# The gate-spreading stage of a PEER decoder layer: first factors made by three engines instead of two

## The chip, the cores and the metric

The kernel runs on one core of a Trainium2 chip. The metric is the device time of one execution, in microseconds (us). Before the change the median of three runs is 3275.36 us (3272.27 to 3279.01). One further execution was profiled; it took 3269.89 us, and its trace is what the rows below come from.

## The reference, cut to what matters

One decoder layer on 1024 tokens: attention (two kinds of heads), then a PEER channel mixer, then a norm. In the mixer each token picks, in each of 8 heads, 16 experts out of 128 x 128. An expert is a pair of keys (i1, i2), and each pick has a gate.

```python
best, flat = lax.top_k(cand.reshape(cand.shape[0], PEER_HEADS, PEER_TOPK * PEER_TOPK), PEER_TOPK)
...
expert = i1 * PEER_NKEYS + i2
gate = jax.nn.softmax(best, axis=-1)
...
act = jax.nn.gelu(jnp.einsum('td,thkd->thk', tc, u_sel).astype(jnp.float32), approximate=False)
return jnp.einsum('thk,thkd->td', (act * gc).astype(tc.dtype), v_emb[ec])
```

The kernel computes the mixer for the last 576 tokens (`TD`) densely, over all 16384 experts. For that it needs, for each of these tokens, a 128 x 128 table of gates that is zero except at the token's 128 picks.

## The kernel before, in words

The program is a row of stages, each with its own instruction streams for TensorE, VectorE, ScalarE, GpSimd and SyncE: projection in, attention, projection out, routing (`route`), the spreading of the gates (`spread_gates`), and the experts (`run_experts`). The change lies in `spread_gates` alone.

`slotT` holds for each dense token three columns over 128 partitions, one partition for each pick: the first key, the second key and the gate. The gate table of a token is the product of two 128 x 128 factors over the picks: `first[pick, i] = gate * (i == first key)` and `second[pick, j] = (j == second key)`. TensorE multiplies them (L1579), one f32 matmul for each token, into PSUM.

The 576 tokens are handled in 72 groups of eight (`OCT`), in a fixed order on every engine. A group of eight goes like this:

- VectorE makes `one` (L1552), the bf16 comparison of a row of numbers `iota_gb` with the first keys, laid out with the token innermost, for all eight tokens. Then `second` (L1557), the f32 comparison with the second keys, 1024 elements. Then `first` for the last four tokens (L1562), `one` times the gate.
- ScalarE makes `first` for the first four tokens (L1589), one instruction for each token, reading `one` with a step and scaling by the gate. It runs one group ahead, and then copies the finished group from PSUM to `gates` (L1599).
- GpSimd does nothing in this stage.

The buffers `one`, `first` and `second` are threefold (`BUFS`), the PSUM banks fourfold. VectorE waits for `first_act` and `first_dve` of three groups ago before `one`, and for the matmuls of three groups ago (`spread_done`) before `second`. TensorE waits for the group's `second_ready`, `first_dve` and `first_act`.

The gate tables leave SBUF in five tiles of 64, 128, 128, 128 and 128 tokens, in two alternating buffers. SyncE sends the first four as each is complete (L1527, after 8, 24, 40 and 56 groups). It then waits for the fourth to land and issues six loads for the next stage: `u_raw` twice, `hn_hi_e`, `hn_lo_e`, `v_raw` twice (L1530 to L1536). The fifth tile is sent after group 72, in two parts: 8 of its 128 columns by SyncE (L1539) and the other 120 by ScalarE (L1612). In `run_experts` SyncE waits for the second part before it loads `rows`, `early`, `tail`, `gain` and the next `v_raw`, and GpSimd waits for it before it starts.

Of the kernel before, what the change touches and what calls it, by code (L numbers as in the profile page):

```python
# [6 lines left out]
P = 128  # L7
# [22 lines left out]
PH, NKEY, PQ, TOPK = 8, 128, 256, 16  # L30
# [32 lines left out]
bf16 = mybir.dt.bfloat16  # L63
i32 = mybir.dt.int32
u32 = mybir.dt.uint32
ALU = mybir.AluOpType
# [1411 lines left out]
def spread_gates(core, slotT, outer):  # L1478

    nc, ps = core.nc, core.ps  # L1480
    OCT = 8
    TU = BANK // NKEY
    NB = OCT // TU
    BUFS = 3
    PS_BUFS = 4
    EDGES = [0, *range(P - HALF_AT, TD + 1, P)]
    NOCT = TD // OCT
    ON_ACT = 4
    LEAD = 8
    with ExitStack() as ctx:  # L1490
        sb, new_sem = core.scope(ctx)
        made = []

        def sem(name):
            made.append(new_sem(name))
            return made[-1]

        with nc.sbuf_tensor("gates1", [P, NKEY, P], f32, side="right") as gates1:
            pass
        lead = Lead(core, outer)  # L1500
        gates = [ctx.enter_context(nc.sbuf_tensor("gates0", [P, NKEY, P], f32, side="right")), gates1]
        one = sb("one", [P, BUFS, NKEY, OCT], bf16)
        first = sb("first", [P, BUFS, OCT, NKEY])
        second = sb("second", [P, BUFS, OCT, NKEY])
        iota_f = core.iota
        iota = sb("iota_gb", [P, NKEY, OCT], bf16)
        keysT = sb("slot_keys", [P, TD], bf16)
        iota_ready, keys_ready = sem("iota_ready_g"), sem("keys_ready_g")
        one_ready, second_ready, first_act, first_dve = (sem(x) for x in (
            "one_ready", "second_ready", "first_act", "first_dve"))  # L1510
        spread_done, gates_out = sem("spread_done"), sem("gates_out")
        sent = [sem(f"gates_sent{k}") for k in range(2)]
        clear_counts(nc, (*made, *lead.semaphores()))
        block = ctx.enter_context(nc.Block())
        flat = slotT

        def need(eng, sem_, value):
            if value > 0:
                eng.wait_ge(sem_, value)

        @block.sync
        def _(sp):
            dst = core.scr_g.rearrange("j i t -> i j t")
            for tile in range(NDT - 1):
                a, b = EDGES[tile], EDGES[tile + 1]
                sp.wait_ge(gates_out, b // OCT)
                sp.dma_start(dst[:, :, a:b], gates[tile % 2][:, :, 0:b - a]).then_inc(sent[tile % 2], 16)  # L1527
            assert NDT % 2 == 1
            sp.wait_ge(sent[1], 16 * (NDT // 2))
            sp.dma_start(lead.u_raw[:, 0, :], core.i["uT"][0]).then_inc(lead.u_in[0], 16)  # L1530
            sp.dma_start(lead.u_raw[:, 1, :], core.i["uT"][1]).then_inc(lead.u_in[1], 16)
            sp.dma_start(lead.hn_hi[:, :, :].bitcast(f32), core.scr_hi).then_inc(lead.hn_in, 16)
            sp.dma_start(lead.hn_lo[:, :, :].bitcast(f32), core.scr_lo).then_inc(lead.hn_in, 16)
            v_v = core.i["v_rows"].rearrange("(i j) d -> j i d", j=NKEY)
            for c in range(CH):
                sp.dma_start(lead.v_raw[:, c, :], v_v[c]).then_inc(lead.v_in[c], 16)  # L1536
            sp.wait_ge(sent[0], 16 * (NDT // 2))
            sp.wait_ge(gates_out, NOCT)
            sp.dma_start(dst[:, 0:LEAD, EDGES[-2]:], gates[0][:, 0:LEAD, :]).then_inc(lead.last_sent[0], 16)  # L1539

        @block.vector
        def _(dve):
            nc.vector.tensor_copy(iota[:, :, :], iota_f[:, :].rearrange("p (i o) -> p i o", o=1)
                                  .to_broadcast([P, NKEY, OCT])).then_inc(iota_ready, 1)
            nc.vector.tensor_copy(keysT[:, :], flat[:, 0, :]).then_inc(keys_ready, 1)
            dve.wait_ge(iota_ready, 1)
            dve.wait_ge(keys_ready, 1)
            for n in range(NOCT):
                b, at = n % BUFS, n * OCT
                need(dve, first_act, n - BUFS + 1)  # L1550
                need(dve, first_dve, n - BUFS + 1)
                nc.vector.tensor_tensor(  # L1552
                    one[:, b, :, :], iota[:, :, :],
                    keysT[:, at:at + OCT].rearrange("p (o t) -> p o t", o=1).to_broadcast([P, NKEY, OCT]),
                    ALU.is_equal).then_inc(one_ready, 1)
                need(dve, spread_done, n - BUFS + 1)
                nc.vector.tensor_tensor(  # L1557
                    second[:, b, :, :], iota_f[:, :].rearrange("p (o i) -> p o i", o=1).to_broadcast([P, OCT, NKEY]),
                    flat[:, 1, at:at + OCT].rearrange("p (t o) -> p t o", o=1).to_broadcast([P, OCT, NKEY]),
                    ALU.is_equal).then_inc(second_ready, 1)  # L1560
                dve.wait_ge(one_ready, n + 1)
                nc.vector.tensor_tensor(  # L1562
                    first[:, b, ON_ACT:, :], one[:, b, :, ON_ACT:].rearrange("p i t -> p t i"),
                    flat[:, 2, at + ON_ACT:at + OCT].rearrange("p (t o) -> p t o", o=1)
                    .to_broadcast([P, OCT - ON_ACT, NKEY]), ALU.mult).then_inc(first_dve, 1)
            for c in range(CH):
                lead.split_u(nc, dve, c)

        @block.tensor
        def _(pe):  # L1570
            for n in range(NOCT):
                b, bank = n % BUFS, NB * (n % PS_BUFS)
                pe.wait_ge(second_ready, n + 1)
                pe.wait_ge(first_dve, n + 1)
                pe.wait_ge(first_act, n + 1)
                need(pe, gates_out, n - PS_BUFS + 1)
                for t in range(OCT):
                    slot = ps[:, bank + t // TU, :].rearrange("p (i t) -> p t i", t=TU)[:, t % TU, :]
                    last = nc.tensor.matmul(slot, first[:, b, t, :], second[:, b, t, :], start=True, stop=True)  # L1579
                last.then_inc(spread_done, 1)  # L1580

        @block.scalar
        def _(act):
            def weight(n):
                b, at = n % BUFS, n * OCT
                act.wait_ge(one_ready, n + 1)
                need(act, spread_done, n - BUFS + 1)
                for t in range(ON_ACT):
                    last = nc.scalar.activation(first[:, b, t, :], one[:, b, :, t], ACT.Copy,  # L1589
# [645 lines left out]
def layer(nc, ins, out):  # L2235
    with ExitStack() as ctx, ExitStack() as outer:
# [24 lines left out]
        with ExitStack() as peer:  # L2261
            eid = peer.enter_context(nc.sbuf_tensor("eid", [P, GT, 2, UNIT], i32))
            eidT = peer.enter_context(nc.sbuf_tensor("eidT", [P, GT, P], i32))
            sgate = peer.enter_context(nc.sbuf_tensor("sgate", [P, GT, 2, UNIT], f32))
            slots = peer.enter_context(ExitStack())
            slotT = slots.enter_context(nc.sbuf_tensor("slotT", [P, 3, TD], f32))
            route(core, hn_hi, hn_lo, w_raw, keys, slotT, eid, eidT, sgate)
            hidden.close()
            lead = spread_gates(core, slotT, peer)
            slots.close()  # L2270
            run_experts(core, eid, eidT, sgate, lead)
# [52 lines left out]
```

## Time and profile before

| what | value |
|---|---|
| median of 3 runs | 3275.36 us |
| profiled execution | 3269.89 us |
| its span | 3268.1 us |
| TensorE busy | 2969.7 us (91%) |
| VectorE busy | 2194.5 us (67%) |
| ScalarE busy | 991.5 us (30%) |
| GpSimd busy | 1262.3 us (39%) |
| matmuls of `spread_gates`, first and last start | 1173.9 and 1368.5 us |

The engines' shares are means over the whole span. The stage of the change covers about 6% of it, so it has to be read in windows of its own. Start to start of consecutive instructions is the time that an engine spends on one: the durations of small instructions overlap, and their sum is more than the time they take.

### The profile page before, as it was taken

To read this page: it belongs to the slowest core of one execution; us is meant where nothing else is said; L and a number is where in the kernel's file an instruction comes from. 1 tells how busy PE (TensorE), PEld (TensorE's weight loads), DVE (VectorE), ACT (ScalarE), POOL (GpSimd) and SP (SyncE) were. 2 spreads that over 40 slices of the span, in tenths; PEclk is the share of its full clock that TensorE was granted. 3 is DMA by queue.
4 is the path that set the end of the run, shared out by engine and by line. 5 is a ranking of instruction groups with operands and counts; after the bars stand their busy time and mean duration, and the time that the engine had idled before them with its cause. 6 is when DMAs were issued, how large, how long until landed. Compare 5 with 4: busy or idle time off the path is not lost.

```text
span 3268.1 us, 52468 instructions
## 1 busy us (share of the span) xinstructions
PE 2969.7 (91%) x19914; PEld 2433.1 (74%) x19914; DVE 2194.5 (67%) x4836; ACT 991.5 (30%) x1668; POOL 1262.3 (39%) x1088
## 2 busy tenths in 40 slices
PE   7997988997888857689999999999999999999997
PEld 4444666545677756689998888888888889888876
DVE  1212544335999879768987777777777777777435
ACT  2223655311223169722222122122222221222212
POOL 0000000000333400024467767666666767675241
PEclk9998999998999989999999999999999999999998
DMA  5213101012112126898899999999999999999684
GB/s 192 100 56 127 40 27 53 35 52 107 56 49 70 51 62 186 258 296 294 283 361 398 373 371 388 376 379 382 379 383 389 378 391 375 380 388 337 223 327 165
DMA packets 330175, 779.24 MB, mean 238 GB/s; under 512 B 45649, under 2 KB 147281, under 8 KB 328529
## 3 DMA queue, kind: packets, MB, share of 16 engines
q0 software_dynamic: 129024, 469.82, 38.0%
q1 hardware_dynamic: 178512, 288.92, 25.4%
q10 hardware_dynamic: 22400, 17.32, 1.6%
q8 instruction: 150, 2.46, 0.3%
q14 instruction: 89, 0.72, 0.1%
HBM read 699.42 MB, written 72.35 MB: 236 GB/s over the span
## 4 chain that ended last, share of the span: by engine, by line
PE 45%; DVE 8%; DMA 5%; issue 4%; POOL 1%; ACT 1%; SPq 0%; DVEq 0%; ACTq 0%
PE psum L1894 20%; PE psum L1878 20%; PE psum L1920 5%; DMA u_ring<-u_rows,eid 3%; DVE first L1562 2%; DVE one L1552 1%; DMA scr_g<-gates 1%; DVE acc L2083 1%; DVE u_ring L2091 1%; POOL v_ring L1851 1%; DVE u_lo L2047 1%; DVE v_lo L2069 1%; DMA v_ring<-v_rows,eidT 1%; DMA v_raw<-v_rows 0%; DVE w_lo L2064 0%
## 5 line engine op out<-in xcount | busy, mean ns | idle before, releaser
L1851 POOL DMA_INDIRECT v_ring<-v_rows,eidT x448 | 594.8, 1328 | 400.0 <-PE psum L1920 290.2
L1843 POOL DMA_INDIRECT u_ring<-u_rows,eid x448 | 516.3, 1152 | 286.6 <-DVE dots L2091 181.3
L2091 DVE CUSTOM_DVE_ANT_0 u_ring<-u_ring,rows 128x1024 f32<-128x1024 f32 x448 | 544.8, 1218 | 114.4 <-DMA u_ring<-u_rows,eid 113.1
L1878 PE MATMUL psum<-hn_hi_e,u_hi 128*128 128x288 f32 x1792 | 531.5, 297 | 14.1 <-DVE w L2059 8.6
L1878 PE MATMUL psum<-hn_lo_e,u_hi 128*128 128x288 f32 x1792 | 529.2, 295 | 0.0
L1878 PE MATMUL psum<-hn_hi_e,u_lo 128*128 128x288 f32 x1792 | 528.9, 295 | 0.0
L1894 PE MATMUL psum<-w_hi,v_hi 128*128 128x288 f32 x2048 | 462.7, 308 | 53.6 <-DVE acc L2083 41.7
L2083 DVE TENSOR_TENSOR acc<-psum,acc 128x576 f32<-128x576 f32 x504 | 379.8, 754 | 140.6 <-PE psum L1894 131.6
L1894 PE MATMUL psum<-w_lo,v_hi 128*128 128x288 f32 x2048 | 446.9, 300 | 0.0
L1894 PEld LDWEIGHTS psum<-w_hi,v_hi 128*128 128x128 f32 x2048 | 334.7, 193 | 150.6 <-issue 99.5
L1894 PE MATMUL psum<-w_hi,v_lo 128*128 128x288 f32 x2048 | 446.0, 300 | 0.0
L1878 PEld LDWEIGHTS psum<-hn_hi_e,u_hi 128*128 128x128 f32 x1792 | 338.3, 189 | 19.7 <-issue 14.0
L1894 PEld LDWEIGHTS psum<-w_lo,v_hi 128*128 128x128 f32 x2048 | 338.2, 193 | 0.0
L1894 PEld LDWEIGHTS psum<-w_hi,v_lo 128*128 128x128 f32 x2048 | 338.1, 193 | 0.0
L1878 PEld LDWEIGHTS psum<-hn_lo_e,u_hi 128*128 128x128 f32 x1792 | 338.1, 189 | 0.0
L1878 PEld LDWEIGHTS psum<-hn_hi_e,u_lo 128*128 128x128 f32 x1792 | 337.9, 189 | 0.0
L1981 ACT ACTIVATE psum<-psum 128x576 f32<-128x576 f32 x112 | 71.1, 635 | 857.8 <-PE psum L1878 857.8
L1992 ACT ACTIVATE v_hi<-v_raw 128x1024 fp32r<-128x1024 f32 x128 | 128.9, 1054 | 390.1 <-PE psum L1894 378.5
L1920 PE MATMUL psum<-v_ring,strip 128*32 128x512 f32 x1792 | 216.9, 602 | 9.4 <-DMA v_ring<-v_rows,eidT 9.4
L2059 DVE TENSOR_TENSOR w<-psum,w 128x576 f32<-128x576 f32 x112 | 84.7, 756 | 207.5 <-ACT psum L1981 189.3
L473 PE MATMUL psum<-w_in,hT 128*128 128x512 f32 (+1 forms) x512 | 212.1, 576 | 0.0
L780 DVE CUSTOM_DVE_ANT_0 sm<-psum,mask 128x256 f32<-128x256 f32 (+7 forms) x128 | 96.2, 752 | 151.9 <-PE psum L675 151.9
(238 smaller groups left out, 4226.7 us busy)
## 6 DMA issues: line engine op xcount, KB each, us to landing
v_raw<-v_rows SPq DMA_DIRECT2D x128, 512.0 KB, 7.4
u_raw<-uT SPq DMA_DIRECT2D x112, 512.0 KB, 8.1
w<-scr_g SPq DMA_DIRECT2D x128, 288.0 KB, 5.9
scr_g<-gates SPq DMA_DIRECT2D x3, 8192.0 KB, 30.7
scr_m<-st_m SPq DMA_DIRECT2D x8, 1024.0 KB, 4.0
w_raw<-in_w_pq SPq DMA_DIRECT2D x8, 1024.0 KB, 6.6
u_raw_r<-uT SPq DMA_DIRECT2D x16, 512.0 KB, 3.6
scr_g<-gates ACTq DMA_DIRECT2D x1, 7680.0 KB, 40.7
```

What stands on the lines that cost most here:

```text
L473: last = nc.tensor.matmul(ps[:, 2 + c, 0:width(c)], hT[:, k, j, :], w_in[:, j, c * BANK:c * BANK + width(c)], start=j == 0, stop=j == KD - 1)
L780: nc.vector.tensor_tensor_reduce(out=sm[:, k, 0:nk], in0=ps[:, 2 * k:2 * k + 2, :].rearrange("p b n -> p (b n)")[:, 0:nk], in1=mask[:, int ...
L1843: pool.indirect_dma_start(u_ring[:, n % U_RING, :], None, core.i["u_rows"], bass.IndirectOffsetOnAxis(eid[:, x // 2, x % 2, k:k + 1], 0)). ...
L1851: pool.indirect_dma_start(v_ring[:, m % V_RING, :], None, core.i["v_rows"], bass.IndirectOffsetOnAxis(eidT[:, x // 2, col:col + 1], 0)).th ...
L1878: last = nc.tensor.matmul(ps[:, a, 0:COLS], x[:, c, j, :], y[:, j, a * COLS:(a + 1) * COLS], start=m == 0, stop=m == len(terms) - 1)
L1894: last = nc.tensor.matmul(ps[:, OUT_AT + F % OUT_PAIRS * 2 + a, 0:COLS], x[:, c, f * P:(f + 1) * P], y[:, b, c, a * COLS:(a + 1) * COLS], ...
L1920: last = nc.tensor.matmul(ps[k * WIDE:(k + 1) * WIDE, SUM_AT + half, :], strip[:, p % 2, at:at + WIDE], v_ring[:, n % V_RING, half * BANK: ...
L1981: nc.scalar.activation(ps[:, 0:ACTS, 0:COLS], ps[:, 0:ACTS, 0:COLS], ACT.Gelu).then_inc(gelu_ready, 1)
L1992: nc.scalar.activation(v_hi[:, c, :], v_raw[:, c, :], ACT.Copy).then_inc(v_hi_ready, 1)
L2059: nc.vector.tensor_tensor(half, ps[:, 0:ACTS, 0:COLS], half, ALU.mult).then_inc(w_ready, 1)
L2083: nc.vector.tensor_tensor(into, ps[:, at:at + 2, 0:COLS], into, ALU.add).then_inc(added, 1)
L2091: nc.vector.tensor_tensor_reduce(out=u, in0=u, in1=rows[:, x % 2, :], scale=1.0, scalar=0.0, op0=ALU.mult, op1=ALU.add, accum_out=dots[:, ...
```

## The change

The eight first factors of a group are divided anew. ScalarE makes those of tokens 0 to 2, from a `one` that now holds only these three (384 elements in place of 1024). GpSimd makes those of tokens 3 and 4, and VectorE those of tokens 5 to 7: each by one `tensor_scalar` from the f32 row of numbers, compared with the key and multiplied by the gate, both read as columns of `slotT` with one value for each partition. TensorE waits for a third semaphore, `first_pool`, and GpSimd for the matmuls of three groups ago. VectorE no longer waits for its own `one_ready`, nor for its own `first_dve` of three groups ago.

```diff
-    ON_ACT = 4
+    ON_ACT, ON_POOL = 3, 2
+    BY_KEY = ON_ACT + ON_POOL
...
-        one = sb("one", [P, BUFS, NKEY, OCT], bf16)
+        one = sb("one", [P, BUFS, NKEY, ON_ACT], bf16)
...
-                need(dve, first_dve, n - BUFS + 1)
                 nc.vector.tensor_tensor(
                     one[:, b, :, :], iota[:, :, :],
-                    keysT[:, at:at + OCT].rearrange("p (o t) -> p o t", o=1).to_broadcast([P, NKEY, OCT]),
+                    keysT[:, at:at + ON_ACT].rearrange("p (o t) -> p o t", o=1).to_broadcast([P, NKEY, ON_ACT]),
                     ALU.is_equal).then_inc(one_ready, 1)
...
-                dve.wait_ge(one_ready, n + 1)
-                nc.vector.tensor_tensor(
-                    first[:, b, ON_ACT:, :], one[:, b, :, ON_ACT:].rearrange("p i t -> p t i"),
-                    flat[:, 2, at + ON_ACT:at + OCT].rearrange("p (t o) -> p t o", o=1)
-                    .to_broadcast([P, OCT - ON_ACT, NKEY]), ALU.mult).then_inc(first_dve, 1)
+                for t in range(BY_KEY, OCT):
+                    nc.vector.tensor_scalar(first[:, b, t, :], iota_f[:, :], flat[:, 0, at + t:at + t + 1],
+                                            flat[:, 2, at + t:at + t + 1], ALU.is_equal, ALU.mult).then_inc(first_dve, 1)
...
+        @block.gpsimd
+        def _(pool):
+            for n in range(NOCT):
+                b, at = n % BUFS, n * OCT
+                need(pool, spread_done, n - BUFS + 1)
+                for t in range(ON_ACT, BY_KEY):
+                    nc.gpsimd.tensor_scalar(first[:, b, t, :], iota_f[:, :], flat[:, 0, at + t:at + t + 1],
+                                            flat[:, 2, at + t:at + t + 1], ALU.is_equal, ALU.mult).then_inc(first_pool, 1)
...
                 pe.wait_ge(second_ready, n + 1)
-                pe.wait_ge(first_dve, n + 1)
+                pe.wait_ge(first_dve, (n + 1) * (OCT - BY_KEY))
+                pe.wait_ge(first_pool, (n + 1) * ON_POOL)
                 pe.wait_ge(first_act, n + 1)
```

What stands in a row on VectorE at the start of the stage, before:

```order
L1543 CAST iota_gb<-iota 128x1024
L1545 CAST slot_keys<-slotT 128x576
L1552 TENSOR_TENSOR one<-iota_gb,slot_keys 128x1024
L1557 TENSOR_TENSOR second<-iota,slotT 128x1024
L1562 TENSOR_TENSOR first<-one,slotT 128x512
```

And on VectorE at the same place in the changed kernel:

```order
L1544 CAST iota_gb<-iota 128x384
L1546 CAST slot_keys<-slotT 128x576
L1552 TENSOR_TENSOR one<-iota_gb,slot_keys 128x384
L1557 TENSOR_TENSOR second<-iota,slotT 128x1024
L1562 TENSOR_SCALAR first<-iota,slotT 128x128 x3
```

The last three rows repeat 72 times in both. `one` shrinks to 384 elements, `second` stays as it was, and one instruction of 512 elements becomes three of 128.

On GpSimd, between the end of `route` and the start of `run_experts`, the changed kernel has these rows, where before the branch L1000 was followed by the branch L1833 and the memset of `tail` (an `ISA` row of the same kind stands ahead of GpSimd's first instruction in `route`, in both kernels):

```order
L1567 UNCONDITIONAL_BRANCH
L1573 ISA
L1573 TENSOR_SCALAR first<-iota,slotT 128x128 x144
L1491 UNCONDITIONAL_BRANCH
L1841 UNCONDITIONAL_BRANCH
L1845 MEMSET tail 128x1024
```

GpSimd gets 144 instructions, two for each group, and one `ISA` instruction ahead of the first. Nothing of the later stages moved on it.

## Rows read from the trace of the kernel before

**Rows 1.** Page, the chain of work that ended last: shares by engine and by line.

```profile
PE 45%; DVE 8%; DMA 5%; issue 4%; POOL 1%; ACT 1%; SPq 0%; DVEq 0%; ACTq 0%
```

**Rows 2.** Stretches of the stage and after: length, then busy us of PE, PEld, DVE, ACT, POOL, then clock, DMA share, GB/s.

```profile
1225.00:1275.00 50.00, 36.90 (x292) 34.03 (x293) 50.00 (x57) 49.56 (x92) 0.00 (x0) 1.00 0.60 169
...
1358.00:1370.00 12.00, 8.09 (x64) 7.45 (x64) 10.41 (x12) 11.91 (x20) 0.00 (x0) 1.00 0.92 362
...
1380.00:1390.00 10.00, 3.11 (x21) 2.91 (x21) 0.76 (x1) 0.64 (x1) 0.00 (x0) 0.72 1.10 347
```

**Rows 3.** Timeline, one group of eight: start us, us, engine, line, operation.

```profile
1301.44 0.68 DVE L1552 TENSOR_TENSOR one<-iota_gb,slot_keys 128x1024 bf16<-128x1024 bf16 x1
...
1301.62 2.02 PE L1579 MATMUL psum<-second,first 128*128 128x128 f32 x16 [0.69 <-DVE first L1562]
1302.04 1.21 DVE L1557 TENSOR_TENSOR second<-iota,slotT 128x1024 f32<-128x1024 f32 x1
1302.15 1.79 ACT L1589 ACTIVATE first<-one,slotT 128x128 f32<-128x128 bf16 x4
1303.18 1.06 DVE L1562 TENSOR_TENSOR first<-one,slotT 128x512 f32<-128x512 bf16 x1
1303.84 1.01 ACT L1599 ACTIVATE gates<-psum 128x1024 f32<-128x1024 f32 x1
1304.15 0.68 DVE L1552 TENSOR_TENSOR one<-iota_gb,slot_keys 128x1024 bf16<-128x1024 bf16 x1
```

**Rows 4.** One line each: count, durations in ns (min/median/max), first and last start.

```profile
L1562 DVE TENSOR_TENSOR first<-one,slotT x72: 1046/1063/1100, 1172.8 to 1365.6; 128x512 f32<-128x512 bf16 x72
L1357 DVE TENSOR_TENSOR hit<-at,iota_p x32: 482/737/2089, 813.9 to 1134.3; 128x640 bf16<-128x640 bf16 x16, 128x1600 bf16<-128x1600 bf16 x16
```

**Rows 5.** Small VectorE instructions with a column operand, and how they follow each other.

```profile
246.30 0.35 DVE L402 TENSOR_SCALAR cn<-st_a,rstc 128x256 f32<-128x256 f32 x1
246.57 0.28 DVE L403 TENSOR_SCALAR cn<-st_a,rstc 128x128 f32<-128x128 f32 x1
```

**Rows 6.** A group of VectorE instructions: line, operation, shapes, count, busy us, mean ns.

```profile
L1423 DVE TENSOR_SCALAR top_key<-top_u 128x128 f32<-128x128 uint32 x8 | 1.7, 218 | 0.1
```

**Rows 7.** Groups of GpSimd instructions, the same columns.

```profile
L1268 POOL TENSOR_TENSOR number<-top_key 128x128 f32<-128x128 f32 x8 | 3.3, 413 | 0.6
...
L1278 POOL TENSOR_TENSOR near<-top_key 128x64 f32<-128x64 f32 x8 | 2.4, 305 | 370.5 <-DVEq L1426 370.5
```

**Rows 8.** Timeline in `route`: VectorE and GpSimd side by side, and the same kind apart.

```profile
244.53 0.29 DVE L380 TENSOR_TENSOR rt<-st_a,trig 128x128 f32<-128x128 f32 x1
244.74 0.28 DVE L381 TENSOR_TENSOR rt<-st_a,trig 128x128 f32<-128x128 f32 x1
...
990.46 0.31 POOL L1278 TENSOR_TENSOR near<-top_key 128x64 f32<-128x64 f32 x1 [1.52 <-DVEq L1426]
990.47 0.45 DVE L1268 TENSOR_TENSOR pair<-top 128x128 f32<-128x128 f32 x1
990.84 0.61 DVE L1268 TENSOR_TENSOR pair<-top 128x64 f32<-128x64 f32 x3
```

**Rows 9.** Timeline: one VectorE cast beside a long GpSimd instruction, and one alone.

```profile
986.53 2.40 POOL L1291 TENSOR_TENSOR u_lo_r<-u_raw_r,u_hi_r 128x1024 fp32r<-128x1024 f32 x1 [4.88 <-ACT u_hi_r L1178]
988.20 0.80 DVE L1400 CAST eid<-expert 128x64 f32 x1
...
1159.93 0.20 DVE L1400 CAST eid<-expert 128x64 int32<-128x64 f32 x1
```

**Rows 10.** SyncE's issues: the fourth tile's store, and the first load behind it.

```profile
1326.59 0.36 SPq L1527 DMA_DIRECT2D scr_g<-gates  x1
...
1358.21 0.35 SPq L1530 DMA_DIRECT2D u_raw<-uT  x1
```

**Rows 11.** The chain in order of time: start us, us, what.

```profile
1370.09 40.67 DMA scr_g<-gates
```

**Rows 12.** GpSimd's configuration ahead of its first instruction in `route`.

```profile
L1278 POOLq MODIFY_POOL_CONFIG  x2: 11/11/11, 758.0 to 758.1; - x2
```

More of the change, by code:

```diff
@@ L1505, in spread_gates @@
         iota_f = core.iota
-        iota = sb("iota_gb", [P, NKEY, OCT], bf16)
+        iota = sb("iota_gb", [P, NKEY, ON_ACT], bf16)
         keysT = sb("slot_keys", [P, TD], bf16)
         iota_ready, keys_ready = sem("iota_ready_g"), sem("keys_ready_g")
-        one_ready, second_ready, first_act, first_dve = (sem(x) for x in (
-            "one_ready", "second_ready", "first_act", "first_dve"))
+        one_ready, second_ready, first_act, first_pool, first_dve = (sem(x) for x in (
+            "one_ready", "second_ready", "first_act", "first_pool", "first_dve"))
         spread_done, gates_out = sem("spread_done"), sem("gates_out")
@@ L1543, in _ @@
             nc.vector.tensor_copy(iota[:, :, :], iota_f[:, :].rearrange("p (i o) -> p i o", o=1)
-                                  .to_broadcast([P, NKEY, OCT])).then_inc(iota_ready, 1)
+                                  .to_broadcast([P, NKEY, ON_ACT])).then_inc(iota_ready, 1)
             nc.vector.tensor_copy(keysT[:, :], flat[:, 0, :]).then_inc(keys_ready, 1)
```

## The prediction, made before the changed kernel was run

> **What bounds the kernel now.** I first read the chain of work that ended last. It is mostly TensorE, and VectorE has 8% of it [rows 1]. Since the change is in one stage, I then cut the span into stretches. Between 1225 and 1275 us VectorE is busy for 50.00 of 50 us, ScalarE for 49.56, TensorE for 36.90, GpSimd not at all [rows 2]. So the spreading of the gates is bound by VectorE and ScalarE together, and the 91% of TensorE belongs to other stages.
>
> The timeline of one group of eight tokens shows how the time splits [rows 3]. VectorE starts `one` at 1301.44, `second` at 1302.04, `first` at 1303.18 and the next `one` at 1304.15: 0.60, 1.14 and 0.97 us, 2.71 in all. ScalarE starts four weighted copies at 1302.15 and the copy out of PSUM at 1303.84: 1.69 us, 0.42 for each, which leaves 1.02 of the 2.71 for the copy. TensorE needs 2.02 us and idles for 0.69, released by VectorE's `first`. 72 groups start from 1172.8 to 1365.6 [rows 4], 2.715 us apart. TensorE's granted clock is full (1.00, the 2.4 GHz level) in these stretches [rows 2].
>
> **What the end of the stage looks like.** The fourth tile is sent at 1326.59, after 56 groups; SyncE goes on at 1358.21, when it has landed [rows 10]. Six loads are issued then, and at 1370.09 the fifth tile, which takes 40.67 us to land and is on the chain [rows 11]. Meanwhile the DMA engines' share is 0.92, then 1.10 [rows 2]. From the fourth tile's landing to the fifth's, 52.6 us, they have no slack worth counting. So if the groups get faster, this block moves forward by what 56 groups gain, not 72. What the last 16 gain only sends the fifth tile into a fuller DMA. With slack there, all 72 would count; that is my other bound.
>
> **The change part by part, for one group.**
>
> `one` shrinks from 1024 to 384 elements. A bf16 comparison of 640 elements takes 482 ns at least [rows 4], one of 1024 takes 0.68 us [rows 3]: 0.52 ns for an element. 640 fewer take off 0.335 us, so 0.60 becomes 0.265.
>
> `second` is untouched: 1.14 us, if nothing gets in its way.
>
> `first` on VectorE (0.97 us) goes, and three `tensor_scalar` of 128 elements come. The nearest are L402 and L403, with one column operand: 256 elements take 0.27 us to the next start, and are 0.07 us longer than 128 [rows 5]. That makes 0.20 for 128, and 0.60 for three. These have two column operands. The kind without a column lasts 218 ns [rows 6], the one with a column 0.28 us [rows 5], so a second column costs nothing or another 0.06: 0.20 to 0.26 each, 0.60 to 0.79 for three. I take 0.60, the row's own value. VectorE alone: 0.265 + 1.14 + 0.60 = 2.00 us.
>
> ScalarE loses one weighted copy: 2.71 - 0.42 = 2.29 us. TensorE's 2.02 stays. On the ring of three buffers there is room: a factor is needed again 2.0 us of matmuls after the last one is made.
>
> GpSimd gets two `tensor_scalar` of 128 elements. The trace has none on this engine. Its two-input instruction of 128 elements lasts 413 ns [rows 7], so two take some 0.83 us of a group, far less than the group. By itself GpSimd is no bound: it would take more than 1.1 us for each instruction to become one.
>
> But GpSimd and VectorE get in each other's way, and this is the cost that the diff does not show. In `route` a VectorE addition of 128 elements starts together with a GpSimd one of 64 elements (305 ns, [rows 7]): VectorE's next starts 0.37 us later. Two of the same size alone are 0.21 apart [rows 8]. So a GpSimd instruction of 305 ns cost VectorE 0.16 us. A cast that takes 0.20 us alone took 0.80 beside a GpSimd subtraction, and ended at 989.00, just after it (988.93) [rows 9]. And `hit`, whose median is 737 ns, took 2089 once [rows 4]. So such VectorE instructions wait for a GpSimd one to finish. For 128 elements I add the difference of the GpSimd durations, 413 - 305 = 0.11 us [rows 7]: 0.27 us for each, 0.54 for two. The bounds: nothing, if the two happen not to meet (VectorE's work has hardly a gap, so I do not believe it), and the whole 0.41 each, 0.83 for two, or more if this instruction is slower than the two-input one.
>
> The Trainium skill (SBUF — State Buffer, section "Who interferes with whom") has a rule on this: a VectorE instruction with two SBUF inputs, or in a two-port mode as `tensor_scalar` can be, shares a port pair with GpSimd by an exclusive lock held for the whole instruction, and the later one blocks. By that rule all five VectorE instructions of a group are exposed; rows 9 agree with it, while rows 8 show a net cost smaller than the whole instruction. What it gives if it holds in full is the second rival.
>
> The sum for a group: 2.00 + 0.54 = 2.54 us, against 2.715. Gain 0.175, times 56 groups = 9.8 us (12.6 with 72). At the start of the stage the cast `iota_gb` shrinks with `one`, by about 0.3 us. Together 10.1 us: from 3269.9 of the profiled execution to 3259.8. The median of the runs is 5.5 us above that execution, so I predict 3265.3, say 3265.
>
> One more thing at the start: GpSimd has an `ISA` instruction ahead of its first `tensor_scalar`. Its like in `route` stands at 758.0 us as a configuration of 11 ns [rows 12], with GpSimd's first work long after it, so the trace bounds what it delays only from above. I cost it at nothing, since VectorE can run three groups ahead of TensorE before it must wait. The Trainium skill (GPSIMD Engine Reference, section "Instruction dispatch") puts a first call after such a load at some 6 us; by that the first matmuls would come about 2 us later and the sum would be 3267.
>
> **The rivals.** The change helps or hurts by one balance. Without `one` and `second` (1.405 us), 1.31 us of a group are left for three VectorE `tensor_scalar` and what two of GpSimd's take from VectorE. I forecast 0.60 + 0.54 = 1.14.
>
> - *Hardly any blocking, ScalarE bounds.* If GpSimd's work falls into VectorE's start-up gaps, VectorE needs 2.0 to 2.3 us and ScalarE's 2.29 decides. Gain 0.42 x 56 + 0.3 = 23.9 us: 3251. For it: rows 8 show less than the whole instruction. Against it: the cast of rows 9.
> - *The two costs cancel the gain.* With a second column at 0.06 us, a group is 0.265 + 1.14 + 0.79 + 0.54 = 2.735. With the whole GpSimd instruction lost, 2.00 + 0.83 = 2.83. That gives from 3276 to 3282, around no change. This is also where the rule of the skill leads by itself.
> - *Slower: VectorE waits for GpSimd.* If both come together, 0.265 + 1.14 + 0.79 + 0.83 = 3.02 us for a group: 0.31 x 56 = 17 us more, 3292. Its place is VectorE's `second` and `tensor_scalar`, its price the time that GpSimd holds them up, and it decides as soon as that passes 1.31 us less three VectorE instructions (0.71 to 0.52 us a group). For it: two inputs of which each is a column, and two operations, may make GpSimd's instruction longer than 413 ns. Against it: it reads one tensor, not two.
> - *Nothing changes at the end.* If the DMA share of the tail were what set the end of the stage altogether, the gain would vanish. But the fourth tile takes 31.6 us and there are 43.4 between two tiles, so the stores wait for the groups and not the other way round.
>
> **How the numbers follow.** A measurement of this kernel can tell about 0.2% from no change, 6.6 us. A group must get 0.11 us shorter or longer for that. Forecast, 2.42 to 2.61 us a group: 0.28. Hardly any blocking: 0.17. Cancelled, within 0.2%: 0.27. Slower: 0.28. So faster 0.45, same 0.27, slower 0.28. The likeliest time is 3265; its own range is 3258 to 3270. As cases of both signs hold the chance, the range goes from ScalarE's bound, 3250, to the slow rival, 3293.
>
> **What would show it.** In the changed profile: starts of `second` 2.5 to 2.6 us apart and 72 of them; VectorE busy all the time in the stage and ScalarE with gaps; VectorE's three `tensor_scalar` about 0.20 us apart where GpSimd is idle; GpSimd's at 0.35 to 0.45 us; a few of `second` or `one` lengthened by 0.2 to 0.4. The fifth tile's store should be issued less than 43.5 us after the fourth's, yet take longer than 40.67 us to land. The prediction is wrong if GpSimd's instruction lasts well over 0.5 us, if VectorE's take over 0.26 apart from waits, or if ScalarE turns out to be the engine without gaps.

## The result, and the profile after

The changed kernel is slower: 3290.4 us median of 6 runs (3286.37 to 3291.62), against 3272.23 us (3260.36 to 3279.01, 6 runs) of the kernel before on the same chips. The ratio is 1.0058, with a 95% interval of 1.0039 to 1.0077. The prediction was 3265 us, faster. The measured time lies inside its range, at the end where its slow rival stood.

The stage's window, in the columns of [rows 2], says which engine it is bound by now:

```profile
1225.00:1275.00 50.00, 37.57 (x268) 35.64 (x267) 39.55 (x89) 32.39 (x71) 49.41 (x34) 0.89 0.59 166
```

Before, VectorE was busy for 50.00 of 50 us and GpSimd for nothing. Now VectorE has 39.55, ScalarE 32.39, and GpSimd 49.41. It handled 34 instructions in 50 us, 17 groups of eight, where the kernel before handled 18.4 (50 divided by its 2.715 us a group). TensorE's granted clock fell from 1.00 to 0.89 in this window. Behind some of its pauses of 2.46 us it is at the lower of its two levels, 1.2 GHz, for the matmuls that follow:

```profile
1370.05:1373.46 3.41, 3.41 (x18) 3.41 (x18) 0.03 (x1) 0.03 (x1) 2.90 (x4) 0.50 0.57 135
```

That group's matmuls, from 1369.84 on, take 3.57 us instead of the 2.02 of [rows 3]. It hardly sets the pace: in the whole stage GpSimd waits 3.9 us for TensorE.

The lines of the stage, in the form of [rows 4] (count, ns min/median/max, first and last start):

```profile
L1552 DVE TENSOR_TENSOR one<-iota_gb,slot_keys x72: 408/416/585, 1170.3 to 1379.8; 128x384 bf16<-128x384 bf16 x72
...
L1557 DVE TENSOR_TENSOR second<-iota,slotT x72: 1208/1218/1241, 1170.6 to 1380.2; 128x1024 f32<-128x1024 f32 x72
...
L1562 DVE TENSOR_SCALAR first<-iota,slotT x216: 331/341/428, 1171.8 to 1381.8; 128x128 f32<-128x128 f32 x108
...
L1573 POOL TENSOR_SCALAR first<-iota,slotT x144: 782/1371/2256, 1169.5 to 1384.4; 128x128 f32<-128x128 f32 x144
...
L1607 ACT ACTIVATE gates<-psum x72: 1007/1023/1025, 1176.7 to 1390.6; 128x1024 f32<-128x1024 f32 x72
```

VectorE's `second` lasts what it lasted before (1.21 us in [rows 3]), so GpSimd hardly held it up. GpSimd's instruction is the one that is stretched: 782 ns at least, 1371 in the median, 2256 at most. From the first copy out of PSUM to the last, 71 groups take 213.9 us, 3.01 us each. Before it was 2.70 by the same lines.

The timeline shows how it goes (start us, us, engine, line, operation; first the GpSimd rows, then the VectorE rows of the same stretch):

```profile
1302.78 2.26 POOL L1573 TENSOR_SCALAR first<-iota,slotT 128x128 f32<-128x128 f32 x1
1305.02 2.25 POOL L1573 TENSOR_SCALAR first<-iota,slotT 128x128 f32<-128x128 f32 x1
1307.26 1.02 POOL L1573 TENSOR_SCALAR first<-iota,slotT 128x128 f32<-128x128 f32 x1
1308.27 0.79 POOL L1573 TENSOR_SCALAR first<-iota,slotT 128x128 f32<-128x128 f32 x1
...
1303.07 1.21 DVE L1557 TENSOR_TENSOR second<-iota,slotT 128x1024 f32<-128x1024 f32 x1
1304.20 0.91 DVE L1562 TENSOR_SCALAR first<-iota,slotT 128x128 f32<-128x128 f32 x3
1304.97 0.41 DVE L1552 TENSOR_TENSOR one<-iota_gb,slot_keys 128x384 bf16<-128x384 bf16 x1
1305.31 1.21 DVE L1557 TENSOR_TENSOR second<-iota,slotT 128x1024 f32<-128x1024 f32 x1
1306.44 0.91 DVE L1562 TENSOR_SCALAR first<-iota,slotT 128x128 f32<-128x128 f32 x3
1307.21 0.41 DVE L1552 TENSOR_TENSOR one<-iota_gb,slot_keys 128x384 bf16<-128x384 bf16 x1
1310.26 1.22 DVE L1557 TENSOR_TENSOR second<-iota,slotT 128x1024 f32<-128x1024 f32 x1 [2.64 <-PE psum L1587]
```

VectorE runs its groups 2.24 us apart (1303.07 to 1305.31). In each of them GpSimd finishes one instruction, while a group needs two. So TensorE falls behind and VectorE, at most three groups ahead, stops at 1307.6 for 2.64 us. Only then does GpSimd run at 0.79 us an instruction and catch up. Then the pattern starts again.

The table of waits (1180 to 1360 us) puts TensorE's idle time down to VectorE, because an instruction of VectorE, of a later group, ends within 0.1 us of GpSimd's second one:

```profile
PE psum L1587 <- DVE first L1562: 44.7, 38, 2.5
```

Taken group by group, the trace says otherwise. The group that TensorE starts at 1307.49 had its VectorE factors at 1302.87 and GpSimd's second one at 1307.27. Of TensorE's 51.7 us of idle time between groups, 47.7 end with GpSimd's second factor as the last of the group's factors to be ready, the rest with ScalarE's, none with VectorE's. GpSimd's instructions fill 211.8 of the stage's 215 us.

At the end of the stage, the chain has this row, to be read against [rows 11]:

```profile
1391.67 36.77 DMA scr_g<-gates
```

The fifth tile is sent 21.6 us later than before and lands 17.7 us later (1428.44 against 1410.76). The fourth was sent 15.0 us later (1341.58 against 1326.59) and landed 13.9 us later (1372.13 against 1358.20).

### The profile page after: what moved, and what is told of

Its sections match the earlier page's. It is cut to its first block, busy times and chain, and to the rows that moved or that the text cites. A ratio compares the mean times of both kernels' runs of the same rounds, so it can differ in the third digit from the quotient of the medians.

```text
span 3288.4 us, 52622 instructions
## 1 busy us (share of the span) xinstructions
PE 2987.2 (91%) x19914; PEld 2452.5 (75%) x19914; DVE 2162.5 (66%) x4980; ACT 934.0 (28%) x1596; POOL 1471.6 (45%) x1232
## 3 DMA queue, kind: packets, MB, share of 16 engines
q8 instruction: 150, 2.46, 0.3%
## 4 chain that ended last, share of the span: by engine, by line
PE 45%; DVE 9%; DMA 5%; issue 2%; POOL 1%; ACT 1%; SPq 0%; DVEq 0%; ACTq 0%
PE psum L1902 19%; PE psum L1886 19%; PE psum L1928 5%; DMA u_ring<-u_rows,eid 3%; DVE second L1557 2%; PE psum L1587 2%; DVE first L1562 2%; DMA scr_g<-gates 1%; DVE acc L2091 1%; POOL v_ring L1859 1%; DVE u_ring L2099 1%; DVE u_lo L2055 1%; DVE v_lo L2077 1%; DMA v_ring<-v_rows,eidT 1%; DMA v_raw<-v_rows 0%
## 5 line engine op out<-in xcount | busy, mean ns | idle before, releaser
L2099 DVE CUSTOM_DVE_ANT_0 u_ring<-u_ring,rows 128x1024 f32<-128x1024 f32 x448 | 545.2, 1218 | 105.3 <-DMA u_ring<-u_rows,eid 104.0
L1573 POOL TENSOR_SCALAR first<-iota,slotT 128x128 f32<-128x128 f32 x144 | 211.8, 1483 | 17.5 <-POOLq L108 13.6
L1587 PE MATMUL psum<-second,first 128*128 128x128 f32 x1152 | 165.0, 309 | 59.2 <-DVE first L1562 59.1
```

What stands on the lines that cost most here:

```text
L1573: nc.gpsimd.tensor_scalar(first[:, b, t, :], iota_f[:, :], flat[:, 0, at + t:at + t + 1], flat[:, 2, at + t:at + t + 1], ALU.is_equal, ALU ...
L2099: nc.vector.tensor_tensor_reduce(out=u, in0=u, in1=rows[:, x % 2, :], scale=1.0, scalar=0.0, op0=ALU.mult, op1=ALU.add, accum_out=dots[:, ...
```

## The experiments

Each was run beside the kernel before, on the same chip. Paces are the time from the first to the last start of the copy out of PSUM, divided by 71.

**e1: the instructions apart and side by side.** Ahead of the stage come fourteen short phases on scratch buffers; the table of them:

```diff
+        PHASES = [((p_scalar, 6), None), ((p_fixed, 6), None), ((p_single, 6), None), ((p_tensor, 6), None),
+                  (None, (d_scalar, 6)), (None, (d_wide, 6)), (None, (d_single, 6)), (None, (d_fixed, 6)),
+                  ((p_scalar, 6), (d_scalar, 24)), ((p_scalar, 6), (d_single, 24)), ((p_scalar, 6), (d_tensor, 3)),
+                  ((p_tensor, 6), (d_scalar, 24)), ((p_tensor, 6), (d_tensor, 3)), ((p_memset, 6), (d_tensor, 3))]
```

`scalar` is the two-column form of the change, `single` has one column and one operation, `fixed` two constants, `tensor` two tensors (on VectorE: `second`).

> Fourteen short phases ahead of the stage, on scratch buffers, in which GpSimd and VectorE run the stage's instructions alone and side by side. The stage itself is the changed kernel's. Theory A (GpSimd's reads are shut out while VectorE runs an instruction with two tensor inputs from SBUF): GpSimd's scalar instruction lasts 0.78 us alone and 0.78 us beside VectorE's scalar instructions of one tensor input, and the first of it beside three `second` comparisons lasts about 3.4 + 0.8 us or until the last comparison ends; VectorE's own are not lengthened. Rival B (GpSimd's instruction is slow by itself): 1.4 us alone. Rival C (it is VectorE's scalar instructions that shut it out, as users of both ports): 0.78 us alone and beside `second`, but over 1.5 us beside the scalar ones. Of VectorE alone I expect 0.28 us from start to start for the two-column form; if 256 elements take 0.13 us more than 128, it runs at one element a cycle, if 0.07 more, at two.

Measured (3350.49 us, one run, with the phases in it): GpSimd's instruction, alone, then beside three `second` of VectorE, and GpSimd's two-tensor form beside the same; with VectorE's rows:

```profile
1170.24 0.78 POOL L1526 TENSOR_SCALAR first<-iota,slotT 128x128 f32<-128x128 f32 x1
...
1190.05 0.84 POOL L1526 TENSOR_SCALAR first<-iota,slotT 128x128 f32<-128x128 f32 x1
...
1199.44 2.88 POOL L1526 TENSOR_SCALAR first<-iota,slotT 128x128 f32<-128x128 f32 x1
1202.31 1.41 POOL L1526 TENSOR_SCALAR first<-iota,slotT 128x128 f32<-128x128 f32 x1
1203.70 0.79 POOL L1526 TENSOR_SCALAR first<-iota,slotT 128x128 f32<-128x128 f32 x1
...
1214.24 1.43 POOL L1535 TENSOR_TENSOR first<-iota,slotT 128x128 f32<-128x128 f32 x1 [4.84 <-DVE second L1541]
...
1218.41 0.45 POOL L1535 TENSOR_TENSOR first<-iota,slotT 128x128 f32<-128x128 f32 x1
...
1219.79 3.50 DVE L1553 TENSOR_TENSOR second<-iota,slotT 128x1024 f32<-128x1024 f32 x3 [1.65 <-POOL first L1535]
...
1199.44 3.61 DVE L1553 TENSOR_TENSOR second<-iota,slotT 128x1024 f32<-128x1024 f32 x3 [0.80 <-POOL first L1526]
...
1214.13 4.01 DVE L1553 TENSOR_TENSOR second<-iota,slotT 128x1024 f32<-128x1024 f32 x3
```

GpSimd's two-column instruction lasts 0.78 us alone (the first 1.23) and 0.83 to 1.02 beside VectorE's two-column ones (0.84 in the row at 1190.05), but the first lasts 2.88 beside `second`, which it costs almost nothing: three of them take 3.61 us, against 3.50 beside memsets. Rivals B and C fall. Theory A holds in its direction and not in its size: the first was expected to need 3.4 + 0.8 us or the time until the last comparison ended (1203.05), and it ended at 1202.32, so it was not shut out all the time. The two-tensor form behaves the other way: 0.45 us alone, once through for each `second`, and `second` pays for it (4.01 us for three). By the same phases, GpSimd from start to start: 0.78 with two columns, 0.61 with constants, 0.58 with one column, 0.41 with two tensors. VectorE from start to start: 0.26 with two columns, 0.32 with two columns and 256 elements, 0.20 with one column, 0.14 with constants. So a column costs VectorE 0.06 us, and 128 more elements 0.07.

**e2: the changed kernel without `second` after the first three groups.**

```diff
+                if n >= BUFS:
+                    nc.vector.tensor_tensor(second[:, b, 0:1, 0:8], iota_f[:, 0:8].rearrange("p (o i) -> p o i", o=1), iota_f[:, 0:8].rearrange("p (o i) -> p o i", o=1), ALU.mult).then_inc(second_ready, 1)
+                else: nc.vector.tensor_tensor(
```

> The changed kernel without the comparison `second` after the first three groups (a tiny multiplication of 8 elements stands in its place), so the gates of the later groups are not computed as they should be. Theory A: 1.14 us of the time in which GpSimd is shut out goes from each group; GpSimd needs 2 x 0.78 + 0.27 + about 0.1 = 1.9 us, and TensorE's 2.0 to 2.1 us sets the pace; GpSimd's instruction has a median under 0.9 us. Rival B: GpSimd's instruction stays at 1.4 to 1.5 us and the pace at 3.0 us a group. Rival C: VectorE's scalar instructions are still there, so the median stays over 1.2 us.

Measured: 3238.96 us, one run. The pace is 2.20 us a group, and GpSimd's mean falls from 1476 to 936 ns:

```profile
L1575 POOL TENSOR_SCALAR first<-iota,slotT 128x128 f32<-128x128 f32 x130 | 120.4, 936 | 16.7 <-PE psum L1589 16.7
```

Its idle time now ends with TensorE's matmuls, so it is no longer the bound. It is `second` that stretches GpSimd. The sizes were expected a little smaller: a pace of TensorE's 2.0 to 2.1 us, and a median of GpSimd's instruction under 0.9 us, where it is 1.00.

**e3: GpSimd makes one token, VectorE four.**

```diff
-    ON_ACT, ON_POOL = 3, 2
+    ON_ACT, ON_POOL = 3, 1
```

> GpSimd makes one token's factor instead of two, VectorE four. Theory A: GpSimd needs 0.78 us beside 1.41 us of two-input instructions, 2.19 us, less than VectorE's 0.27 + 1.14 + 4 x 0.28 = 2.53 us, which sets the pace; against before (2.71) 0.19 us a group, 11 to 13 us less: about 3260 us. Rival B: GpSimd's 1.4 us would fit as well, the same pace; this run does not tell A from B, but shows that GpSimd's second instruction is what costs. Rival C: over 2.7 us a group, no gain.

Measured: 3260.2 us, ratio 0.9970 (0.9957 to 0.9983), pace 2.48. VectorE is without a gap, as forecast.

```profile
L1573 POOL TENSOR_SCALAR first<-iota,slotT 128x128 f32<-128x128 f32 x64 | 157.9, 2472 | 2.2 <-PE psum L1587 0.2
```

GpSimd's one instruction lasts 2.47 us here, the whole of VectorE's group: as long as VectorE does not stop, it gets one through. Giving it half the work turns 18 us slower into 8 us faster.

**e4: `second` by eight scalar instructions.**

```diff
-                nc.vector.tensor_tensor(
...
+                for t in range(OCT):
+                    nc.vector.tensor_scalar(second[:, b, t, :], iota_f[:, :], flat[:, 1, at + t:at + t + 1],
+                                            None, ALU.is_equal).then_inc(second_ready, 1)
...
-                pe.wait_ge(second_ready, n + 1)
+                pe.wait_ge(second_ready, (n + 1) * OCT)
```

> `second` is made by eight scalar instructions with one column each in place of one two-input comparison; the rest is the changed kernel. VectorE alone then needs 0.27 + 8 x 0.20 + 0.84 = 2.7 us. Theory A: GpSimd is shut out for 0.27 us only and fits its two instructions in; the pace is VectorE's 2.7 us, as before the change, although VectorE does more: within 5 us of the kernel before, some 18 us less than the changed one. Rival B: 2.97 to 3.0 us, as the changed kernel. Rival C: GpSimd is shut out nearly always: far slower, over 3.5 us a group, 3330 us or more.

Measured: 3271.1 us, ratio 1.0009 (0.9995 to 1.0023), pace 2.79, with no gap on VectorE.

```profile
L1572 POOL TENSOR_SCALAR first<-iota,slotT 128x128 f32<-128x128 f32 x100 | 104.5, 1051 | 36.0 <-PE psum L1586 36.0
```

GpSimd needs 0.86 and 1.23 us for its two and then waits for TensorE. VectorE's time for a group went up by 0.55 us, from 2.24 to 2.79 (0.12 of it is more than its own spacings add up to, 0.34 + 8 x 0.196 + 3 x 0.256 = 2.67), and yet the kernel is 15 us faster than the changed one, each taken against the kernel before (+2.8 against +18.2).

**e5: ScalarE four, GpSimd one, VectorE three.**

```diff
-    ON_ACT, ON_POOL = 3, 2
+    ON_ACT, ON_POOL = 4, 1
```

> ScalarE makes four tokens' factors, GpSimd one, VectorE three. VectorE needs 0.33 + 1.14 + 3 x 0.27 = 2.3 us a group, ScalarE 1.02 + 4 x 0.30 = 2.2 us if its read of `one` at a step of 8 bytes costs what it costs at 6 (2.7 us if it costs what it cost at 16). GpSimd fits one instruction into each of VectorE's groups. Theory A: 2.3 us a group, 23 us less than before the change: about 3246 us. If ScalarE's reading step is the dearer one: 2.7 us, no change.

Measured: 3241.6 us, ratio 0.9916 (0.9897 to 0.9936), pace 2.32. It beats both kernels: 28.6 us less than before. ScalarE's read at a step of 8 bytes lasts 401 ns, near the 392 at 6 bytes and far from the 519 of before. GpSimd gets its one instruction through in each group and then waits for TensorE:

```profile
L1573 POOL TENSOR_SCALAR first<-iota,slotT 128x128 f32<-128x128 f32 x62 | 119.1, 1921 | 21.9 <-PE psum L1587 21.9
```

**e6: ScalarE four, GpSimd none, VectorE four.** The GpSimd block and the wait on `first_pool` are gone.

```diff
-    ON_ACT, ON_POOL = 3, 2
+    ON_ACT, ON_POOL = 4, 0
```

> ScalarE four, GpSimd none, VectorE four. The new VectorE instruction and the packed `one` without GpSimd: VectorE 0.33 + 1.14 + 4 x 0.27 = 2.55 us a group against 2.71 before. Expected 0.16 us x 56 to 72 groups, 9 to 12 us less than before: about 3258 us. If GpSimd's presence were what costs VectorE, as the prediction had it, this would be faster than e3, where VectorE also makes four; by theory A it is slower than e3 by 0.06 us a group (the larger `one`), 3 to 4 us.

Measured: 3256.48 us, ratio 0.9961 (0.9946 to 0.9976), pace 2.48. The ratio overlaps e3's, so the two cannot be told apart, and the 0.06 us for the larger `one` is not there: 512 elements last 417 ns and 384 last 416. Against e5 it says what GpSimd is worth here: one token on GpSimd instead of VectorE saves 15 us.

**e7: `second` in two halves, between the scalar instructions.**

```diff
+                    if t < BY_KEY + 2:
+                        h = (t - BY_KEY) * HALF_OCT
+                        nc.vector.tensor_tensor(
+                            second[:, b, h:h + HALF_OCT, :],
+                            iota_f[:, :].rearrange("p (o i) -> p o i", o=1).to_broadcast([P, HALF_OCT, NKEY]),
+                            flat[:, 1, at + h:at + h + HALF_OCT].rearrange("p (t o) -> p t o", o=1)
+                            .to_broadcast([P, HALF_OCT, NKEY]), ALU.is_equal).then_inc(second_ready, 1)
```

> The changed kernel with `second` made in two halves of four tokens, and VectorE's instructions in the order one, scalar, half, scalar, half, scalar. VectorE alone: 2.24 + 0.07 = 2.31 us. Theory A in its finer form (a GpSimd scalar instruction needs the shared read path several times, for each column and for the row, and each time waits for the two-input instruction of the moment): more and shorter two-input instructions let it through more often, but each one's wait is shorter too; if it gets two through in each of VectorE's groups, the pace is 2.3 us, and some 23 us less than before. In its coarse form (GpSimd gets only the time in which no two-input instruction runs, 0.78 us for each instruction): 1.47 + 2 x 0.78 = 3.0 us as in the changed kernel, or worse, since the gaps of 0.27 us are shorter than 0.78.

Measured: 3256.17 us, ratio 0.9955 (0.9940 to 0.9971), pace 2.44, between the 2.3 of the finer form and the 3.0 of the coarse one. The same division of work as the changed kernel, 32 us apart from it when each is taken against the kernel before.

```profile
L1577 POOL TENSOR_SCALAR first<-iota,slotT 128x128 f32<-128x128 f32 x115 | 141.1, 1239 | 0.0
```

GpSimd now gets two instructions through in each of VectorE's groups (1.38 and 1.10 us), and VectorE pays for it: `one` lasts 0.50 us instead of 0.41. The coarse form of theory A falls: what counts is not only the time that VectorE's two-input instructions leave, but how that time is cut. (The order of VectorE's instructions was changed with it, and the two were not run apart.)

**e8 to e12: other instructions on GpSimd, two for each group as in the change.** e8, with two constants:

```diff
-                    nc.gpsimd.tensor_scalar(first[:, b, t, :], iota_f[:, :], flat[:, 0, at + t:at + t + 1],
-                                            flat[:, 2, at + t:at + t + 1], ALU.is_equal, ALU.mult).then_inc(first_pool, 1)
+                    nc.gpsimd.tensor_scalar(first[:, b, t, :], iota_f[:, :], 3.0, 2.0, ALU.is_equal, ALU.mult).then_inc(first_pool, 1)
```

In the others the same two lines are replaced: in e9 by two tensors, in e10 by one column, in e11 by two columns and 32 elements, in e12 by one column and 256 elements, written to a buffer of its own. In e11 and e12 GpSimd also zeroes its part of `first` ahead of the stage. None of the five computes the gates as the kernel has to.

```diff
+                    nc.gpsimd.tensor_tensor(first[:, b, t, :], iota_f[:, :], flat[:, 0, 0:P], ALU.mult).then_inc(first_pool, 1)
```

```diff
+                    nc.gpsimd.tensor_scalar(first[:, b, t, :], iota_f[:, :], flat[:, 0, at + t:at + t + 1], None, ALU.is_equal).then_inc(first_pool, 1)
```

```diff
+                    nc.gpsimd.tensor_scalar(first[:, b, t, 0:32], iota_f[:, 0:32], flat[:, 0, at + t:at + t + 1],
+                                            flat[:, 2, at + t:at + t + 1], ALU.is_equal, ALU.mult).then_inc(first_pool, 1)
```

```diff
+        aside = sb("aside", [P, BUFS, ON_POOL, 2 * P])
...
+                    nc.gpsimd.tensor_scalar(aside[:, b, t - ON_ACT, :], flat[:, 1, 0:2 * P], flat[:, 0, at + t:at + t + 1], None, ALU.is_equal).then_inc(first_pool, 1)
```

> The changed kernel with GpSimd's two column operands replaced by two constants, so two of each eight first factors are not computed as they should be. By the phases GpSimd's instruction then takes 0.61 us alone instead of 0.78. If it is the reading of columns that waits for VectorE, each instruction needs the shared path once, two get through in each of VectorE's groups of 2.24 us, and the pace is 2.24 to 2.3 us. If only the time matters that VectorE's two-input instructions leave (coarse form): 1.41 + 2 x 0.61 = 2.6 us.

> The changed kernel with GpSimd's two scalar instructions replaced by two multiplications of two tensors, 128 elements each, the instruction whose row the prediction used for the price; two of each eight first factors are not computed as they should be. In the phases this kind lasted 0.45 us alone (0.41 from start to start), and beside `second` it went through once for each comparison and lengthened it by 0.26 us. If the prediction's step on the blocking was right for this kind, VectorE is slowed by 0.26 us for each one that meets it: 2.24 + 0.26 to 2.24 + 0.52 = 2.5 to 2.76 us a group, with VectorE busy all the time and GpSimd waiting. If the kind of GpSimd's instruction does not matter, 3.0 us.

> The changed kernel with GpSimd's instructions using one column and one operation (the comparison alone, the gate left out), so two of each eight first factors lack their gate. It takes 0.59 us alone, less than the constants' 0.61, but reads a column. If each column that is read means one more wait for VectorE's two-input instructions, its pace lies between that with constants (2.34 us a group) and the changed kernel's (3.01), near 2.6. If only the length of GpSimd's instruction mattered, it would be at or below 2.34.

> The changed kernel with GpSimd's two-column instruction cut from 128 to 32 elements, so three quarters of two of each eight first factors stay zero. It separates the number of columns from the length. If the two columns are what keeps GpSimd to one instruction for each of VectorE's groups, the pace stays near 3.0 us a group even though the instruction is shorter alone (0.6 to 0.7 us). If the length decides, two get through and the pace falls to VectorE's own, 2.24 to 2.35 us.

> The changed kernel with GpSimd's instruction reading one column but 256 elements, into a scratch tensor, so two of each eight first factors are zero. Alone it should last 0.7 to 0.8 us, about what the two-column instruction of 128 elements lasts (0.78). If the columns decide, two get through in each of VectorE's groups and the pace is 2.3 us as with one column and 128 elements (e10). If the length decides, 2.9 to 3.0 us, as in the changed kernel.

| run | GpSimd alone, us | pace, us | one run, us | who is held up |
|---|---|---|---|---|
| changed kernel | 0.78 | 3.01 | | GpSimd |
| e8 constants | 0.61 | 2.33 | 3255.32 | GpSimd, and VectorE by some 0.09 a group |
| e10 one column | 0.58 | 2.30 | 3246.62 | GpSimd, and VectorE by 0.05 a group |
| e11 two columns, 32 elements | 0.46 at least | 2.29 | 3244.38 | GpSimd |
| e12 one column, 256 elements | not run apart, 1.20 at least | 2.58 | 3265.24 | both |
| e9 two tensors | 0.41 | 2.70 | 3272.87 | VectorE |

Two GpSimd instructions go through in each of VectorE's groups in e10 and e11, with almost no idle time on GpSimd:

```profile
L1573 POOL TENSOR_SCALAR first<-iota,slotT 128x128 f32<-128x128 f32 x123 | 141.7, 1171 | 0.0
```

```profile
L1576 POOL TENSOR_SCALAR first<-iota,slotT 128x32 f32<-128x32 f32 x126 | 140.0, 1183 | 1.5 <-PE psum L1590 1.5
```

The rows of e9 and e12 that show VectorE paying:

```profile
1301.77 0.69 DVE L1552 TENSOR_TENSOR one<-iota_gb,slot_keys 128x384 bf16<-128x384 bf16 x1
...
1303.52 1.07 DVE L1562 TENSOR_SCALAR first<-iota,slotT 128x128 f32<-128x128 f32 x3
```

```profile
L1559 DVE TENSOR_TENSOR second<-iota,slotT 128x1024 f32<-128x1024 f32 x55 | 77.6, 1411 | 0.0
```

e9 gives the kernel that the prediction had in mind: GpSimd's instruction of 0.41 us, VectorE's `one` at 0.69 instead of 0.41 and its three scalar ones at 1.07 instead of 0.91, together 0.44 us a group against the 0.54 forecast; the pace, 2.70, is that of before. e10 came out better than expected (2.30, not 2.6): one column does not cost a wait of its own. e11 speaks against the number of columns as the cause (two columns go through twice a group if the instruction is short), and e12 against the length as the only one (1.20 us go through twice a group, but then VectorE is held up). e12 was meant to have the length of the changed kernel's instruction (0.7 to 0.8 us expected alone); at 1.20 us and more it overshot that, and its 2.58 fits neither of the two values that were expected, 2.3 and 2.9 to 3.0. What decides which of the two engines is held up stays open: a rule would have to give GpSimd the loss for the two-column form, VectorE for two tensors, and both for the long one.

## Why the prediction was wrong

**Where the stage is bound before: right. How much the end counts: right for e3 to e7, and here partly by luck.** The stage became 0.32 us a group slower by the copies out of PSUM; times the forecast's 56 groups that is 17.9 us, the fifth tile landed 17.7 later, and the medians are 18.2 apart. But the block of loads did not move as a whole. The fourth tile landed only 13.9 us later (the stage also began 1.1 us earlier), and from its landing to the fifth's it took 56.3 us in place of 52.6: the fifth tile was sent 21.6 us later, so here a part of what the last 16 groups lose counts too. In e3 to e7 the block keeps its length, 52.3 to 52.9 us.

**"The nearest are L402 and L403 ... 0.20 for 128": a term mis-sized.** The three scalar instructions are 0.256 us apart, at the upper end of the 0.20 to 0.26 that was given; the sum took the lower end. e1 splits it: two operations with constants 0.14, one column 0.20, two 0.26. The rows of the constant form and of the column form [rows 5, 6] together already showed the price of a column. `one` came to 0.34 instead of 0.265: 384 elements in rows of three cost what 512 in rows of four cost (e6). VectorE alone needs 0.34 + 1.14 + 3 x 0.256 = 2.24 us, not 2.00. With that and the forecast's own 0.54 of blocking the sum would have been 2.78, a little slower than before.

**"Its two-input instruction of 128 elements lasts 413 ns": a term mis-sized.** The two-column instruction lasts 0.78 us alone, nearly twice the row that was taken, though it reads one tensor less. (The prediction named "well over 0.5 us" as a sign that it is wrong.) Two of them are still far below a group (1.56 us). What made them the bound is the next step.

**"Such VectorE instructions wait for a GpSimd one to finish" and "By itself GpSimd is no bound": the step that failed.** Rows 8 and 9 show that waiting for GpSimd's two-tensor instructions, and e9 confirms it for them, in size too (0.46 us for two, by the pace, against 0.54). For the scalar form with two columns it is GpSimd that waits: `second` kept its 1218 ns and GpSimd's instruction went from 0.78 us to 1.48 in the mean, 2.97 us for the two of a group, which is the pace of 3.01. The prediction read rows of VectorE's side only and priced what VectorE does to GpSimd at nothing. The trace of before shows the other side too, on GpSimd's largest line (count, ns min/median/max, first and last start), and beside it VectorE's `hit`:

```profile
L1308 POOL TENSOR_TENSOR found<-hit,number x16: 2935/2964/3713, 816.8 to 1153.5; 128x1600 f32<-128x1600 bf16 x16
...
815.65 2.08 DVE L1357 TENSOR_TENSOR hit<-at,iota_p 128x1600 bf16<-128x1600 bf16 x1
...
816.84 3.69 POOL L1308 TENSOR_TENSOR found<-hit,number 128x1600 f32<-128x1600 bf16 x1
```

Seven of these 16 take 3.69 to 3.71 us, and each of the seven starts while such a `hit` is still running; the others take 2.94 to 2.97. In the same seven places `hit` takes 2.08 us instead of 0.98, so its 2089 ns of [rows 4] was not "once" but seven times in 16, and its median of 737 mixes two shapes. There both engines lose, GpSimd 0.7 us of 3.0: a reason to bound GpSimd's stretching as well.

The rule of the Trainium skill (SBUF — State Buffer, section "Who interferes with whom") says whichever comes second blocks, so it covers both directions. The trace of the changed kernel does not bear out that the order decides: GpSimd's instruction of 1302.78 is the earlier one, VectorE's `second` starts beside it at 1303.07 and keeps its 1.21 us, and it is GpSimd's that takes 2.26. The same section puts `tensor_scalar` in a two-port mode among the instructions that exclude GpSimd as well. e1 does not show that at the length of a whole instruction: 128 more elements cost 0.07 us there, 1.9 elements a ns against the 0.85 of `second` (1024 in 1208 ns), so they are in a faster mode, and yet GpSimd's instruction goes through beside them in 0.83 to 1.02 us, while VectorE's are never more than 0.31 us apart.

**The slow rival had the right time for the wrong reason.** It gave 3.02 us a group and 3292 us, by VectorE waiting for GpSimd. Measured are 3.01 and 3290, by GpSimd waiting for VectorE. That the number fits is luck. What would have told them apart was named: "VectorE busy all the time". It was busy for 39.55 of 50 us.

**ScalarE's bound, 2.29 us: too high.** Its read of `one` at a step of 6 bytes lasts 392 ns, against 519 at 16 bytes, so it needs some 1.9 us a group (three starts 0.29 apart and 1.02 for the copy). That is the reserve that e5 uses.

**The `ISA` instruction: nothing, as costed.** GpSimd's first scalar instruction starts at 1169.54, 0.1 us after the configuration at 1169.4, and lasts 1.24 us. The 6 us for a first call that the Trainium skill gives (GPSIMD Engine Reference, section "Instruction dispatch") do not show.

## What to carry to other kernels

Where two engines get in each other's way, price both directions: what the one loses, and how long the other's instruction becomes beside it. Work put on GpSimd beside a VectorE that is busy without a gap with two-input instructions may get through only at VectorE's pace, here one instruction for each 2.24 us though it needs 0.78, so give it no more than that (e3, e5), or cut VectorE's long instructions (e7). And an operand layout that only one engine seems to use can be the cheaper gain: packing `one` gave ScalarE a quarter of its instruction back.

## What the runs showed of the hardware that was not expected

- GpSimd's scalar instruction of 128 elements takes 0.78 us with two column operands, 0.61 with two constants, 0.58 with one column and one operation; its two-tensor multiplication takes 0.41 to 0.42.
- Beside three `second` comparisons, the first two-column instruction lasted 2.88 us and they were lengthened by 0.11 in all; the two-tensor ones lasted 1.43 each and lengthened them by 0.51.
- VectorE's scalar instructions of one tensor let GpSimd's through (0.83 to 1.02 us instead of 0.78) and are hardly slowed (24 in 6.45 us, some 0.2 us in all more than at their spacing alone, 0.26), although they run at 1.9 elements a ns.
- GpSimd memsets do not disturb `second` at all (3.50 us for three).
- TensorE's granted clock in the window fell from 1.00 to 0.89 when its pauses grew from 0.7 to as much as 2.46 us; after the start of the stage, seven groups' matmuls took 3.4 to 3.65 us instead of 2.02.
